# Mixing products in pairs of output tiles from seven half products in place of eight, and another order of VectorE's steps in the first unit of a SwiGLU

## What is computed

```python
x = layer_norm(ALPHA * x + 0.5 * swiglu(x, ffn1_wg, ffn1_wu, ffn1_wd), ln1_g, ln1_b)
z = jnp.einsum('btd,de->bte', x, w_in)                 # D_IN = 5632 = 44 tiles of 128
c_g, b_g, h, p, g_a, g_p = jnp.split(z, SPLITS, axis=-1)
u = c_g * h
y_a = b_g * short_conv(u_ext, conv_w, t_new)           # three taps
q = multiscale_pool(p_ext, pos0, t_new)                # mean of 2, 4, 8, 16 rows, less p
y_p = einsum('btgc,gce->btge', q, pool_w) * pool_scale
m = jax.nn.sigmoid(g_a) * y_a + jax.nn.sigmoid(g_p) * y_p
x = layer_norm(ALPHA * x + jnp.einsum('btd,de->bte', m, w_out), ln2_g, ln2_b)
x = layer_norm(ALPHA * x + 0.5 * swiglu(x, ffn2_wg, ffn2_wu, ffn2_wd), ln3_g, ln3_b)
```

## Time and profile before

| what | value |
|---|---|
| time, median of 3 runs | 1044.84 us (1044.74 to 1045.28) |
| the profiled execution: its own time, and its span | 1046.54 us, 1044.7 us |
| TensorE busy | 1031.5 us (99%), 8592 matmuls |
| VectorE, ScalarE, GpSimd busy | 711.8 (68%), 482.5 (46%), 460.4 us (44%) |
| share of the chain that ended last | PE 93%, DVE 3%, issue 1%, DMA 1% |
| moved by DMA | 103.32 MB, mean 99 GB/s |

### The profile page before, as it was taken

One profiled execution on the slowest core, in us unless ns is written; L12 is line 12 of the kernel. 1 busy time (PEld: TensorE's weight loads), 2 busy tenths in 40 slices (PEclk: granted clock), 3 DMA queues, 4 the chain that ended last, 5 costly groups with the idle time before them and its releaser, 6 DMA issues.

```text
span 1044.7 us, 21275 instructions
## 1 busy us (share of the span) xinstructions
PE 1031.5 (99%) x8592; PEld 1026.5 (98%) x8592; DVE 711.8 (68%) x1144; ACT 482.5 (46%) x735; POOL 460.4 (44%) x358
## 2 busy tenths in 40 slices
PE   8999999999999999999999999999999999999997
PEld 7999999999999999999999999999999999999997
DVE  6987977898755845822524325789888788977276
ACT  3665535645554452332332324456653565456335
POOL 4333444344348354844553546332425433443530
PEclk9999999999999999999999999999999999999999
DMA  8133343334327210532342334203333332432502
GB/s 256 52 102 102 102 121 87 103 97 122 112 83 195 82 40 13 156 103 85 87 117 67 113 89 127 67 14 102 91 112 102 102 116 77 132 101 82 144 20 82
DMA packets 195829, 103.32 MB, mean 99 GB/s; under 512 B 5188, under 2 KB 194260, under 8 KB 195725
## 3 DMA queue, kind: packets, MB, share of 16 engines
q1 hardware_dynamic: 195651, 101.86, 33.9%
q10 hardware_dynamic: 82, 0.12, 0.1%
HBM read 99.74 MB, written 2.48 MB: 98 GB/s over the span
## 4 chain that ended last, share of the span: by engine, by line
PE 93%; DVE 3%; issue 1%; DMA 1%; ACT 0%; SPq 0%; POOL 0%; DVEq 0%; ACTq 0%; POOLq 0%
PE ps L1641 19%; PE ps L1642 19%; PE ps L1643 19%; PE ps L1664 10%; PE ps L1661 10%; PE ps L1662 10%; PE ps L1710 2%; PE ps L1717 1%; PE ps L1711 1%; PE ps L1785 1%; DMA xrow<-in_x_prompt_dram 1%; PE ps L1764 1%; PE ps L2123 0%; DVE xl L1087 0%; DMA raw<-in_ffn_wg_dram 0%
## 5 line engine op out<-in xcount | busy, mean ns | idle before, releaser
L672 POOL TENSOR_TENSOR wl<-raw,wh 128x512 fp32r<-128x512 f32 (+1 forms) x168 | 223.9, 1362 | 328.7 <-DVE raw L1147 313.0
L719 ACT ACTIVATE wh<-raw 128x1024 fp32r<-128x1024 f32 (+4 forms) x183 | 210.4, 1154 | 175.0 <-DMA raw<-in_ffn_wg_dram 57.8
L1642 PE MATMUL ps<-form_lo,wh 128*128 128x260 f32 x640 | 181.5, 284 | 0.0
L1643 PE MATMUL ps<-form_hi,wl 128*128 128x260 f32 x640 | 181.3, 283 | 0.0
L1641 PE MATMUL ps<-form_hi,wh 128*128 128x260 f32 x640 | 181.3, 283 | 0.0
L1661 PE MATMUL ps<-xh,wh 128*128 128x260 f32 x640 | 166.9, 282 | 0.0
L1662 PE MATMUL ps<-xl,wh 128*128 128x260 f32 x640 | 166.5, 282 | 0.0
L1641 PE MATMUL ps<-xh,wh 128*128 128x260 f32 x536 | 152.1, 284 | 2.8 <-POOL wl L672 2.1
L1642 PE MATMUL ps<-xl,wh 128*128 128x260 f32 x536 | 151.8, 283 | 0.0
L1643 PE MATMUL ps<-xh,wl 128*128 128x260 f32 x536 | 151.5, 283 | 0.0
L659 POOL TENSOR_TENSOR wl<-raw,wh 128x512 fp32r<-128x512 f32 x63 | 88.0, 1396 | 138.9 <-ACT wh L719 138.8
(11 more groups left out here) (288 smaller groups left out, 2478.5 us busy)
## 6 DMA issues: line engine op xcount, KB each, us to landing
raw<-in_ffn_wg_dram SPq DMA_DIRECT2D x80, 256.0 KB, 3.3
raw<-in_w_in_dram SPq DMA_DIRECT2D x40, 512.0 KB, 4.0
b<-in_ffn_wu_dram SPq DMA_DIRECT2D x40, 256.0 KB, 3.4
raw<-in_ffn_wu_dram SPq DMA_DIRECT2D x40, 256.0 KB, 3.0
raw<-in_ffn_wd_dram SPq DMA_DIRECT2D x16, 512.0 KB, 5.5
raw<-in_ffn_wd_dram SPq DMA_DIRECT2D x24, 256.0 KB, 3.5
raw<-in_ffn_wd_dram SPq DMA_DIRECT2D x24, 192.0 KB, 2.9
raw<-in_w_out_dram SPq DMA_DIRECT2D x7, 512.0 KB, 3.8
```

Of the source, the lines that this page charges most:

```text
L672: nc.gpsimd.tensor_tensor(slots(wl_slot, s, p), slots(raw_slot, s, p), slots(wh_slot, s, p).bitcast(F32), ALU.subtract).then_inc(lo_ready, 1)
L719: return nc.scalar.activation(out, in_, ACT.Copy)
L1642: mm(out, hi, vl, start=False, stop=False, skip_group_check=more)
L1643: ins = mm(out, lo, vh, start=False, stop=n == count, skip_group_check=more)
```

## The change

The 40 products of the mixing after the opening become 20 units of two output tiles each, listed in `MIX`: `CH` is a tile of C and of H, `GB` a gate tile and one of B, `GG` two tiles of the pooled gate, `BP` and `PP` hold tiles of p. Each is made as a SwiGLU unit is, from seven half products. So the stage has 20 units of 84 matmuls where it had 40 products of 48. The pooled products stay 48 matmuls in all. VectorE gets the sums and rests for 20 more units, and forms of x for this stage. In return ScalarE takes over copies of p and the first tap of the convolution, and GpSimd the window sums (`window_sums`), the rest of q (`q_rest`) and the rest of m (`m_rest`). The opening's fourth tile is a gate (GA) instead of B.

```diff
+    MIX = [None, ("BP", 0), ("GG", 0), ("CH", 1), ("GB", 1), ("CH", 2), ("GB", 2), ("GG", 1), ("PP", 1), ("CH", 3),
+           ("GB", 3), ("CH", 4), ("GB", 4), ("GG", 2), ("CH", 5), ("GB", 5), ("CH", 6), ("GB", 6), ("GG", 3),
+           ("CH", 7), ("GB", 7)]
+    POOLED = {1: (0, 0), 2: (0, 1), 6: (1, 0), 7: (1, 1), 12: (2, 0), 13: (2, 1), 17: (3, 0), 18: (3, 1)}
+    WINDOWS_IN, Q_IN = {3: 1, 10: 2, 14: 3}, {4: 1, 11: 2, 16: 3}
...
-        DOWN_AT = (8, 10, 0, 2, 12, 4, 6, 8)
-        OUT_AT = (10, 12, 6, 8, 4, 0, 2)
+        DOWN_AT = (8, 10, 12, 6, 0, 2, 4)
+        OUT_AT = (8, 10, 12, 6, 0, 2, 4)
...
+            def first_mix_unit():
+                products_u(0, (bank(2, 0), bank(2, 1)), up_sum)
+                t_two(MIXING, 2)
+                pooled_q(0)
+                rest_thirteen(MIXING, 2)
+                last_sum(MIXING, 2)
+                other_taps(0)
+                dve.wait_ge(conv_made, 1)
+                dve.wait_ge(c_copied, 2)
+                tt(two(ymix[:]), two(ymix[:]), pair_of(3), ALU.mult).then_inc(b_taken, 1)
+                kept_first(1)
+                sum_first(1)
+                rest_twenty_four(MIXING, 2)
...
+            def mix_unit(p):
+                sum_second(p - 1)
+                if p < MU:
+                    weight_sums(MIXING, p + 1)
+                    t_two(MIXING, p + 1)
+                    last_sum(MIXING, p + 1)
+                mixed_first(p - 1)
+                if p < MU:
+                    rest_thirteen(MIXING, p + 1)
+                mixed_second(p - 1)
+                if p in Q_IN:
+                    pooled_q(Q_IN[p])
+                kept_first(p)
+                sum_first(p)
+                if p < MU:
+                    rest_twenty_four(MIXING, p + 1)
...
+            for p in range(1, MU + 1):          # GpSimd
+                if p < MU:
+                    split_unit(MIXING, p + 1)
+                if p in M_MADE:
+                    m_rest(M_MADE[p])
+                if p in WINDOWS_IN:
+                    window_sums(WINDOWS_IN[p])
...
+                    if p == 1:                  # TensorE, pooled(p)
+                        pe.wait_ge(b_taken, 1)
...
-                if n == 1:                      # VectorE, norm_steps, after tile 3
-                    weight_sums(1, 1)
-                    t_two(1, 1)
-                    last_sum(1, 1)
+                if not last:
+                    weight_sums(NEXT[n], 1)
+                    t_two(NEXT[n], 1)
+                    last_sum(NEXT[n], 1)
```

826 lines of the change are left out of this document (525 added, 301 removed).

## The result

The changed kernel takes **1059.95 us** in the median of 4 runs (1056.44 to 1064.17), the kernel before 1044.79 (4 runs, 1044.36 to 1045.28): ratio **1.0139, 95% interval 1.0118 to 1.0160**. It is slower by 15 us where the prediction had it faster by 16. The profiled execution took 1060.8 us, its span 1058.9 against 1044.7 before. The 8352 matmuls are there.

A forecast was written before the change was run, and what follows sets the result against it. TensorE, busy for 99% of the span, was taken as the bound; -28.7 + 3.4 - 2.6 + 6.8 + 4.1 - 0.5 + 1.6 + 0.2 = -15.7 from 1044.84 gave 1029.1 us, range 1022 to 1037 (chance 0.63).

The forecast's parts named there:

- The matmuls: In the mixing: 240 fewer matmuls at 0.1198 us each, 28.7 us less.
- The first normalisation: VectorE makes the first mixing unit's sums between tiles 3 and 4, so TensorE waits 1.7 us, plus 1.7 for the clock: +3.4.
- The clock's fall: Behind a wait of about a microsecond or more the granted clock falls to its lower level: 1.7 us added.
- The upper bound of 6.0: First normalisation's upper bound, 4.3 + 1.7, if the three sums each wait for GpSimd as well.
- The second normalisation: w_out's slots and the load come free earlier, tiles end 3.0 us earlier, TensorE's 0.9 us wait and low clock go: -2.6.
- The turn of the first w_out product: At w_out, two products end together and the third waits for VectorE to have read the first: +0.2.
- The entry: In the mixing's first unit TensorE waits 4.1 us for VectorE to free bank pair 3, with ScalarE and clock: +6.8.
- The other units: The 20 mixing units: VectorE keeps up on average but is late in units 4, 10 and 15: +4.1.
- break-even: In each mixing CH unit `sum_second` ends at 12.9 us, just when TensorE wants it.
- SwiGLU: VectorE's reordered first units: the first SwiGLU gains 0.5 us, the second waits longer for `up_second`, costing 1.6.
- B: Rival: VectorE and GpSimd meet at every turn, units at 13 and entry at 8.8, giving 1040 us; chance 0.15.
- C: Rival: slower than before, VectorE becomes the bound of the mixing stage, 1068 us at 60 meetings; chance 0.05.

The follow-up runs named there:

- e5: Changed kernel with VectorE's q, other taps and the product freeing the pooled product's bank ahead of T2, T4 and unit 2's rests at the mixing's entry: 1055.44 us, ratio 1.0094.
- e10: e3 with the two shift sums back within w_out's second product, as in the kernel before, instead of its third: 1057.42 us, ratio 1.0122.
- e2: Changed kernel with the last unit's sigmoid and last m tile's rounding ahead of the roundings of w_out's fourth and fifth product on ScalarE: 1055.64 us, ratio 1.0073.
- e3: e2 with TensorE ending w_out's first product before the second is begun, as in the kernel before: 1056.56 us, ratio 1.0089.
- e11: Changed kernel with e5, e10 (with it e2 and e3), e6, e9 and the old order of the SwiGLU's first unit together: 1040.27 us, ratio 0.9952.
- e14: e11 with T2, T4 and the rest of T1 and T3 behind the second half's statistics, rest of T2 and T4 at the normalisation's end: 1033.67 us, ratio 0.9878.
- e1: Kernel before with only the new order of VectorE's steps in the first unit of both SwiGLUs: 1047.79 us, ratio 1.0029.
- e7: Changed kernel with GpSimd making only 64 of 512 columns of the rests in mixing units 3 to 20: 1054.13 us, ratio 1.0092.
- e4: Changed kernel with the next first unit's weight sums, T2 and T4 behind the first half's statistics, in both normalisations: 1065.88 us, ratio 1.0208.
- e6: Changed kernel with the roundings and rests of the mixing's third and fourth opening product behind those of the last down products: 1063.52 us, ratio 1.0154.
- e9: Changed kernel with the next first unit's three weight sums between the first half's normalisation and the second half's statistics: 1059.29 us, ratio 1.0125.
- e8: Changed kernel with GpSimd's window sums of groups 1 to 3 made for 8 columns only: 1056.13 us, ratio 1.0085.

## Why the prediction was wrong, by its own steps

- **The matmuls, -28.7:** right.
- **The first normalisation, +3.4: the first step that failed; it was 11.5.** The queue on VectorE was the right mechanism. Two sizes were off. The three sums were priced at their mean in the units, 2.6 us, and took 5.6 beside GpSimd's rests of the last down products. And GpSimd's queue itself was left out: the new slots give the fourth down product slot 6, its rest began at 320.98 where before it began at 319.57, and TensorE waited 2.1 us for those of the last two. The clock's fall, priced at 1.7, cost 6.2 in this execution: the 113 matmuls from the statistics (356.18) to the opening (374.90) took 18.7 us, before 12.5. The upper bound of 6.0 was passed by 5.5; in e5, with the same steps and no fall of the clock, the term was 5.4.
- **The second normalisation, -2.6; it was +2.2.** The argument was that w_out's slots, and so SwiGLU 2's weights, come free earlier. They did: VectorE no longer waits for a load there. But VectorE took up the first product at 642.86 where before it was 632.79, 10 us later, by the next step's failure. And its steps between are longer beside GpSimd (2.89 and 3.41 us, the rows under e10), which the term left out. e2 and e3, with the first cause eased, wait 0.6 us and nothing; e10 waits 3.2 again; e11 and e14, with the sums gone from there, wait for nothing. How the loss divides between the two stays open.
- **The turn of the first w_out product, +0.2; w_out was +7.3.** I looked for a wait on the turn and not at what had been put into another order around it. Three things: the sigmoid behind a rounding in ScalarE's queue (2.1 us for ml, a low clock); the shift sums moved from the second into the third product, which leaves 24 matmuls ahead of the tails and not 72 (2.9 us); two products that end together (0.4 us). e2 shows the first; e10 shows where the second comes from, though the time did not come back with it alone.
- **The entry, +6.8; it was +10.2.** The place and the chain were right (`ymix`, L1842, 5.6 us, in its first unit), and e5 shows it. Its length was 15.6 and not 12.3 us, ScalarE's 1.0 counted: 0.9 at the forms, 1.0 at ScalarE, and steps beside GpSimd. TensorE waited 8.0 us in three pieces and not 5.1.
- **The other units, +4.1; it was +10.3.** Right in kind, and the three units that were named waited what was forecast: 4, 10 and 15 together 4.2 us against 4.1. Two sizes were put at nothing without a reason: units 11 and 16, which carry a q too (the forecast charged the q of unit 4 alone), waited 2.9 us; and the clock, which was granted at 0.62 for 4 us behind unit 4's wait and stayed at 1.00 behind the other four, cost about 2 us. A little over 1 us is left open. The taps' mean is 1179 ns where the forecast of break-even had 1000, and yet the CH units without q or window sums (their taps stand in units 6, 12, 17 and 20) made TensorE wait nowhere. VectorE is busy for 82% of the 19 units, below the 85 to 90 expected, and still late where it matters; the mixing took 226.3 us where 218 was forecast. With GpSimd's rests cut 7.7 of the 10.3 us went. The rule of the Trainium skill that I had weighed (SBUF — State Buffer, Who interferes with whom) spoke for a term nearer 13, and the measured 10.3 is nearer to that than to 4.1.
- **SwiGLU, -0.5 and +1.6:** right within 0.7 us by the traces (e1 too); by e1's ratio the two cost 2 to 4 us together. The 1.85 us moved behind `up_second`'s chain are the wait of 2.1.

**Of the rivals**, B (VectorE and GpSimd meet at every turn) had the mechanism and too small a price, 1040: it was confined to the units and the entry, while the same meetings at the two normalisations and the queues at w_out cost more. C did not happen; no stage was bound by VectorE's total work. The range's upper end was built from meetings in the mixing alone. That was the error of method: the terms were bounded by how often a known thing happens, and none held an order on a queue that I had not followed (ScalarE's at the stage's end, the shift sums' place).

**What stays open:** the waits for `sum_second`, 7.2 us in e14; e7 shows that in the changed kernel all but 1.3 of 7.1 us are meetings with GpSimd's rests of weights, alone or beside its window sums, and no order was found that avoids them. And the clock's share, which varies from run to run; see below.

## What to carry to other kernels

Fewer matmuls pay in full only inside a stage; at its two ends write down each engine's queue in order, for every step that the change moved or put behind another, and ask what stands at its head. One sigmoid of 0.37 us behind a rounding that waited for a slot's load was worth some 7 us here, by the ratios of the changed kernel and e2. In these traces a VectorE step with two inputs in SBUF could take as long as the GpSimd instruction beside it, or longer, however small it was, so price it at that and not at the mean, and release GpSimd's work (here by T4) when VectorE's short chains are over: e14, which moved that release and the rests of the sums behind them, is 6.6 us faster than e11. And a wait that goes when a queue is eased is no gain until the next wait on the same queue is looked at: it moved in e4, e6, e9 and e10.

## What the runs showed of the hardware

The granted clock behind a wait is not the same from one execution to the next. At the first statistics TensorE waits 2.55 us in the changed kernel and in e5 with the same code up to there. TensorE alone, in the 14 us behind that wait in both:

```profile
356.00:370.00 14.00, 13.82 (x73) 0.51 0.13 38
```

```profile
357.00:371.00 14.00, 13.80 (x124) 1.00 0.26 76
```

In the first the clock stood at its lower level (1.2 GHz) for the whole stretch, in the second it never left 2.4 GHz, and the stage took 61.2 and 55.1 us. In e8, again with the same code up to there, it was 0.77 in the mean of the 14 us behind the wait, and the stage took 57.8. So one wait of this size cost 0 to 6 us, and not the 1.7 of the earlier trace rows. The runs of the changed kernel lie 7.7 us apart, those of the kernel before beside them 0.9, though in one later comparison its runs lay 7.8 apart too. So a stage of one profile is compared with another's only when the clock agrees, and close 1 above is to be read in this light: 55.1 to 61.3 us is one order of steps under different clocks.

That a step of four columns can take as long as the GpSimd instruction beside it (1.2 us, e11's rows above) I had not expected either; the forecast priced meetings at steps of 512 columns only. The trace of the kernel before had it already: of L1589's steps of 8 columns the one at 396.00, beside GpSimd, took 1.26 us, the one at 482.40 took 0.22.
